# A two-layer hybrid decoder on one core: last sums of the output projection in other banks, earlier copies at the joint, and a plane of four added squares

## What is computed

```
def _layer(x, ...):
    x = _layer_norm(ALPHA * x + 0.5 * _swiglu(x, ffn1...), ln1_g, ln1_b)      # FFN 1, LN1
    xp, q, k, v, xq, gates = jnp.split(x @ w_in, SPLITS, axis=-1)
    ...                      # causal pooling, sliding-window GQA with sinks, cross attention
    merged = sum of sigmoid(gate_b) * (branch_b @ w_br_b) over three branches
    x = _layer_norm(ALPHA * x + merged @ w_o, ln2_g, ln2_b)                   # output projection, LN2
    x = _layer_norm(ALPHA * x + 0.5 * _swiglu(x, ffn2...), ln3_g, ln3_b)      # FFN 2, LN3

def _layer_norm(x, g, b):
    mu = jnp.mean(x, axis=-1, keepdims=True)
    var = jnp.mean(jnp.square(x - mu), axis=-1, keepdims=True)
    return (x - mu) * lax.rsqrt(var + LN_EPS) * g + b
```

## Time and profile before

| what | value |
|---|---|
| time, median of 3 runs | 2475.97 us (2474.82 to 2476.84) |
| the profiled execution's own time | 2475.46 us |
| its span (first to last instruction) | 2472.5 us |
| mean granted TensorE clock | 0.988 of full speed |
| busy share PE / PEld | 97% / 95% |
| busy share DVE / ACT / POOL | 66% / 49% / 25% |
| DMA, mean over the span | 89 GB/s |

### The profile page before, as it was taken

The page is one execution under the profiler, slowest core; times in us unless marked ns, Lnnn a source line. Parts: engine busy times, 40 slices in busy tenths (PEclk is TensorE's granted clock), DMA queues, the critical chain, the costliest instruction groups (busy, mean ns, idle before and its releaser), DMA issues.

```text
span 2472.5 us, 45123 instructions
## 1 busy us (share of the span) xinstructions
PE 2406.2 (97%) x17595; PEld 2341.8 (95%) x17595; DVE 1622.5 (66%) x2744; ACT 1221.0 (49%) x2472; POOL 623.5 (25%) x576
## 2 busy tenths in 40 slices
PE   8999999999999899999999999999999998999997
PEld 8999999899999899999999999989999998999997
DVE  4877776635344587777677777664453457877775
ACT  5555655334322465655565656553443225655654
POOL 1233334120000223333423333341100002333333
PEclk9999999989999999999999999999999999999999
DMA  6222233221122212222213222333112231232231
GB/s 229 93 95 95 95 103 123 77 75 50 61 85 86 86 65 91 89 99 96 93 60 107 93 103 78 112 105 109 43 57 69 86 103 51 73 105 97 84 106 56
DMA packets 54178, 221.29 MB, mean 89 GB/s; under 512 B 15856, under 2 KB 18800, under 8 KB 40880
## 3 DMA queue, kind: packets, MB, share of 16 engines
q1 hardware_dynamic: 53968, 218.41, 26.0%
HBM read 213.58 MB, written 6.04 MB: 89 GB/s over the span
## 4 chain that ended last, share of the span: by engine, by line
PE 79%; DVE 12%; ACT 5%; DVEq 2%; issue 1%; POOL 1%; DMA 0%; ACTq 0%; SPq 0%; POOLq 0%
PE pair L1943 12%; PE pair L1945 11%; PE pair L1944 11%; PE pair L1786 9%; PE pair L1790 9%; PE pair L1788 9%; PE S L1943 2%; PE S L1945 2%; PE S L1944 2%; DVE htl L1202 2%; DVE TP L1122 1%; PE S L2057 1%; ACT hth L743 1%; PE TP L2117 1%; PE S L1897 1%
## 5 line engine op out<-in xcount | busy, mean ns | idle before, releaser
L1943 PE MATMUL pair<-xth,hiA 128*128 128x288 f32 x1216 | 358.6, 295 | 0.4
L1944 PE MATMUL pair<-xtl,hiA 128*128 128x288 f32 x1216 | 358.8, 295 | 0.0
L1945 PE MATMUL pair<-xth,loA 128*128 128x288 f32 x1216 | 358.4, 295 | 0.0
L695 ACT ACTIVATE hiA<-TP 128x512 fp32r<-128x512 f32 (+1 forms) x372 | 194.0, 555 | 205.0 <-DVE TP L1127 125.0
L1691 POOL TENSOR_TENSOR loB<-rawB,hiB 128x512 fp32r<-128x512 f32 (+1 forms) x128 | 161.1, 1259 | 493.6 <-ACT hiB L695 493.5
L1113 DVE TENSOR_TENSOR loA<-TP,hiA 128x512 fp32r<-128x512 f32 (+1 forms) x372 | 235.7, 634 | 17.0 <-ACT hiA L695 14.2
L1108 DVE TENSOR_TENSOR loA<-rawA,hiA 128x1024 fp32r<-128x1024 f32 x96 | 119.1, 1242 | 181.9 <-ACT hiA L682 181.2
L1943 PEld LDWEIGHTS pair<-xth,hiA 128*128 128x128 f32 x1216 | 228.0, 188 | 1.1 <-DVE loA L1113 1.1
L1691 POOL TENSOR_TENSOR loB<-rawA,hiB 128x512 fp32r<-128x512 f32 (+1 forms) x120 | 143.3, 1194 | 340.1 <-ACT hiB L695 340.1
L1945 PEld LDWEIGHTS pair<-xth,loA 128*128 128x128 f32 x1216 | 228.7, 188 | 0.0
L1944 PEld LDWEIGHTS pair<-xtl,hiA 128*128 128x128 f32 x1216 | 228.3, 188 | 0.0
(11 more groups left out here) (388 smaller groups left out, 7046.5 us busy)
## 6 DMA issues: line engine op xcount, KB each, us to landing
rawA<-in_wblk SPq DMA_DIRECT2D x104, 512.0 KB, 3.5
rawA<-in_wg SPq DMA_DIRECT2D x44, 1024.0 KB, 4.8
rawB<-in_wg SPq DMA_DIRECT2D x44, 1024.0 KB, 4.7
rawB<-in_wd SPq DMA_DIRECT2D x24, 768.0 KB, 4.1
rawA<-in_wd SPq DMA_DIRECT2D x24, 768.0 KB, 4.4
rawA<-in_wt_d SPq DMA_DIRECT2D x4, 1024.0 KB, 4.8
rawB<-in_wt_d SPq DMA_DIRECT2D x4, 1024.0 KB, 4.7
mcs<-in_mks SPq DMA_DIRECT2D x2, 2048.0 KB, 11.9
```

Of the source, the lines that this page charges most:

```text
L695: nc.scalar.activation(slot((hiA, hiB), prod, n), src, ACT.Copy).then_inc(f_hi, 1)
L1943: nc.tensor.matmul(bank, wt_hi, xt[0], start=start, stop=False, skip_group_check=True)
L1944: nc.tensor.matmul(bank, wt_hi, xt[1], start=False, stop=False, skip_group_check=True)
L1945: last = nc.tensor.matmul(bank, wt_lo, xt[0], start=False, stop=i == n - 1, skip_group_check=True)
```

## The change

Six edits, all of order, banks or splitting; what is computed stays the same.

1. The memory tokens come in four pieces; the first weight block after the first piece, the second after the fourth. ACT and DVE follow.
2. POOL's add_squares adds the two first sums to one plane (after a drain) and announces only that and 4+5; PE's variance has four matmuls instead of five.
3. At the joint (u == HEADS) ACT's copy_u3 stands ahead of round_hidden(fb, 1, 0) and DVE's sum of c22 ahead of the rest of that hidden plane.
4. Attention: v's transposes go behind project(Q_IN + 3, 0), and the first group's callback comes after chunk 6.
5. Output projection: half 1 of m = 6 and 7 goes to S and TP; residual(4,1) goes ahead of the reciprocal, (5,1) and (6,1) take the places after chunks 1 and 4, (7,1) alone stays at the end. PE's head of FFN 2 waits for the banks only at group 1, and for earlier reads of them.
6. At LN2, PE's mean of half 1 goes into block (1,0,0) after chunk 2 and the variance of half 1 from block (1,0,0) to block (1,1,0), after chunk 5.

```diff
-SQUARE_SUMS = (0, 2, 4)
+SQUARE_SUMS = (0, 4)
...
-            return pair[m % 2][:, 0, 0:TH] if h else (S, TP)[m % 2][:, 1, 0:TH]
+            return (S, TP)[m % 2][:, 1, 0:TH]
...
-            for s in range(2):
-                sp.dma_start(mem[:, 4 * s:4 * s + 4, :], mem0[:, 4 * s:4 * s + 4, :]).then_inc(mem_in[s], 16)
-                sp.dma_start(raw[:, s, :], wblk[s]).then_inc(raw_in[s], 16)
+            for i in range(4):
+                sp.dma_start(mem[:, 2 * i:2 * i + 2, :], mem0[:, 2 * i:2 * i + 2, :]).then_inc(mem_in[i], 16)
+                if i in (0, 3):
+                    sp.dma_start(raw[:, i // 3, :], wblk[i // 3]).then_inc(raw_in[i // 3], 16)
...
-                    if old:
-                        act.wait_ge(f_done, done(fb, u - 1, "P7"))
-                        nc.scalar.activation(u3[:, :], al[(u - 1) % 2], ACT.Copy).then_inc(al_act, 1)
+                    def copy_u3(v):
+
+                        act.wait_ge(f_done, done(fb, v, "P7"))
+                        nc.scalar.activation(u3[:, :], al[v % 2], ACT.Copy).then_inc(al_act, 1)
+
+                    if old and u > HEADS + 1:
+                        copy_u3(u - 1)
...
                     if u == HEADS:
+                        copy_u3(u)
                         round_hidden(fb, 1, 0)
...
+                    if u == HEADS:
+                        sum_c22(u)
...
                     tail_onto_x(fb - 1, 0, 1)
+                else:
+                    residual(4, 1)
                 reciprocal(l, n, 0)
...
-                        residual(4 + c // 4, 1)
+                        residual(5 + c // 4, 1)
...
-                    residual(6, 1)
                     residual(7, 1)
...
-                for c in SQUARE_SUMS:
+                for c in (0, 2, 4):
                     pool.wait_ge(sq_ready, norm_count(l, n, h, c + 1))
-                    nc.gpsimd.tensor_tensor(squares(c), squares(c), squares(c + 1), ALU.add).then_inc(sq_sum, 1)
+                    last = nc.gpsimd.tensor_tensor(squares(c), squares(c), squares(c + 1), ALU.add)
+                    if c == 2:
+                        pool.drain()
+                        last = nc.gpsimd.tensor_tensor(squares(0), squares(0), squares(2), ALU.add)
+                    if c > 0:
+                        last.then_inc(sq_sum, 1)
...
-                    elif f == 1 and g == 0:
-                        pe.wait_ge(pair_free[w], n_use(fb // 2, Q_WO + 3) + 2)
+                    elif f == 1 and g == 1:
+                        pe.wait_ge(pair_free[w], n_use(fb // 2, Q_WO + 2) + 2)
...
-                        if fb and (g, w, h, c) == (1, 0, 0, 5):
+                        if n == 1 and (g, w, h, c) == (1, 0, 0, 2):
+                            mean(l, n, 1)
+                        if fb and (g, w, h, c) == ((1, 1, 0, 5) if n == 1 else (1, 0, 0, 5)):
                             variance(l, n, 1)
...
-                    if fb and h == 0:
+                    if n == 2 and h == 0:
                         mean(l, n, 1)
...
+                project(l, pq(l, Q_IN + 3), 0, n_use(l, Q_IN + 3))
                 pe.wait_ge(pair_free[1], n_use(l, Q_IN + 2) + 2)
...
-                project(l, pq(l, Q_IN + 3), 0, n_use(l, Q_IN + 3))
                 project(l, pq(l, Q_IN + 3), 1, n_use(l, Q_IN + 3))
...
-                        project(l, pq(l, Q_IN + 4), i, n_use(l, Q_IN + 4), between)
+                        project(l, pq(l, Q_IN + 4), i, n_use(l, Q_IN + 4), between, 6 if i == 0 else 4)
...
-                            pe.wait_ge(half_added, l * 4 + m - 5)
+                            pe.wait_ge(half_added, l * 4 + m - 3)
```

More of the change, by code:

```diff
@@ L314, in build @@
         cst_in, x_in, par_in = sem("cst_in"), sem("x_in"), sem("par_in")
-        mem_in = [sem("mem_in0"), sem("mem_in1")]
+        mem_in = [sem(f"mem_in{i}") for i in range(4)]
         raw_in = [sem("raw_in0"), sem("raw_in1")]
@@ L704, in fill_head @@
                     if s == EXTRA:
-                        act.wait_ge(mem_ready, 2)
+                        act.wait_ge(mem_ready, 4)
                     elif s < 4:
@@ L746, in _ @@
             nc.scalar.activation(small[:, 60:61], small[:, 61:62], ACT.Copy)
-            for s in range(2):
-                act.wait_ge(mem_in[s], 16)
-                cs = slice(4 * s, 4 * s + 4)
+            for i in range(4):
+                act.wait_ge(mem_in[i], 16)
+                cs = slice(2 * i, 2 * i + 2)
                 nc.scalar.activation(memh[:, cs, :], mem[:, cs, :], ACT.Copy).then_inc(mem_hi, 1)
-                round_w(0, s)
+                if i in (0, 2):
+                    round_w(0, i // 2)
             for s in range(2):
@@ L1159, in _ @@
             nc.vector.memset(small[:, 60:62], 1.0).then_inc(small_set, 1)
-            for s in range(2):
-                cs = slice(4 * s, 4 * s + 4)
-                dve.wait_ge(mem_hi, s + 1)
+            for i in range(4):
+                cs = slice(2 * i, 2 * i + 2)
+                dve.wait_ge(mem_hi, i + 1)
                 nc.vector.tensor_tensor(meml[:, cs, :], mem[:, cs, :], memh[:, cs, :].bitcast(F32), ALU.subtract).then_inc(mem_ready, 1)
-                rest_w(0, s)
+                if i in (0, 2):
+                    rest_w(0, i // 2)
             for i in range(1, PAIR_MEM):
@@ L1269, in ffn, with sum_c22 @@
                     r, r_old = u % 2, (u - 1) % 2
-                    if g_old:
-                        dve.wait_ge(al_act, 2 * g_count(fb, u - 1))
+                    def sum_c22(v):
+                        dve.wait_ge(al_act, 2 * g_count(fb, v))
                         dve.drain()
-                        nc.vector.tensor_tensor(c22[:, :], u3[:, :], de[r_old], ALU.add).then_inc(de_read, 1)
+                        nc.vector.tensor_tensor(c22[:, :], u3[:, :], de[v % 2], ALU.add).then_inc(de_read, 1)
+                    if g_old and u > HEADS + 1:
+                        sum_c22(u - 1)
                     if d_old:
@@ L1806, in begin, with project @@
                     pe.wait_ge(pair_free[s], u + 1)
-            def project(l, qq, s, u, halfway=None):
+            def project(l, qq, s, u, meanwhile=None, after=4):
                 begin(qq, s, u)
                 for c in range(KC):
-                    if c == KC // 2 and halfway:
-                        halfway()
+                    if c == after and meanwhile:
+                        meanwhile()
                     last = mm3(lambda h: pair[s][:, h, 0:TH], wt(s, c), (xs(xh, c), xs(xl, c)), c, KC)
@@ L1854, in _ @@
                     for c in range(KC):
-                        pe.wait_ge(mem_ready, c // 4 + 1)
+                        pe.wait_ge(mem_ready, c // 2 + 1)
                         last = mm3(lambda h: pair[s][:, 0, 0:N_MEM], wt(s, c, split_of(2 * l)),
```

## The result

The changed kernel takes 2497.16 us (median of 4 runs, 2494.46 to 2499.39) against 2475.39 us before: a ratio of 1.0088, 95% interval 1.0074 to 1.0101, so slower by 22 us (0.9%). The direction is the one forecast, the size is not: +12.1 was forecast, and the range ended at 2495.

A forecast was written before the change was run, and what follows sets the result against it. PE was taken as the bound (79% of the chain's span). Terms -0.4 + 5.3 + 1.6 - 3.8 + 5.4 + 4.0 = +12.1 on 2475.46 gave 2487.6, said as 2488, range 2471 to 2495.

The forecast's parts named there:

- Start and attention: First weight block behind less memory traffic, -0.4; attention's waits for tmp and prob filled, -1.9 in each of two layers, -3.8.
- Joint: P4's wait for u3 goes, but DVE's longer chain delays the next c22: +0.4 at four joints, +1.6.
- Squares: Variances of the norms: one matmul less, but POOL's u comes 0.95 later at six sites PE waits at; together +5.3.
- Head of FFN 2: Mean 3.1 earlier, then PE waits 4.1 for POOL's rests; second reciprocal 2.7 later per layer, +5.4 at full clock.
- Clock: Half rate behind the new 4.1 wait in FFN 2's head: +2.0 in each of two layers, +4.0.
- (a): Rival: same chain, but the clock stays at 2.4 GHz behind the new wait; 2484 (2483 to 2485), chance 0.20.
- (b): Rival: rests of quarters 2 and 3 are there when PE reaches block (1,1,0); -13.8, 2474, chance 0.08.
- (c): Rival: the joints keep their gain, P3's c22 not bound by the chain; -6.0 instead of +1.6, 2480, chance 0.11.
- (d): Rival: every edit gains what it removes, all 27.6 gone; 2448, chance 0.03.

The follow-up runs named there:

- run with the rests ahead: Changed kernel with ACT's rounding and POOL's rests of quarters 2 and 3 put ahead of LN2's second squares: 2483.72 us (1.0033).
- old joint: Changed kernel with edit 3 undone (copy of u3 and sum of c22 at their old places): 2495.58 us (1.0086).
- old head: Changed kernel with edits 5 and 6 undone (old banks, old places of residuals, mean and variance of LN2's second half): 2488.68 us (1.0057).
- plane-alone kernel: Kernel before with edit 2 alone (plane of four squares): 2492.36 us (1.0063).

## Why the prediction was right and wrong

- **Start and attention** (-0.4 and -3.8): right about the waits. In the changed kernel's trace the attention wins 4.35 over both layers. Alone, the two edits measured -2.1, an interval that includes no change, since half-rate stretches in the attention moved; that stood only in the bounds.
- **Joint** (+1.6): right that no gain comes, and in size 0.4 at three of four FFNs by the traces; +1.6 when undone, which the medians alone do not tell from 0. The forecast had one follower that waits 2; there are two that wait 1 each.
- **Squares** (+5.3): the step that failed most. The latency was there: "u comes 0.95 later" holds (415.06 against 414.31 in the earlier trace rows, with POOL starting 0.18 earlier). What failed is "PE's end is POOL's u plus the same three matmuls as before": those matmuls ran at half clock at three of the four first halves of LN1 and LN3 and at the end of the last norm. Before, PE took the sums one by one as they came, so its longest idle piece there was 0.9; with one plane it stands idle 2.4 to 2.6 at a stretch. The clock was weighed at the head of FFN 2 alone, and at the squares not at all. Also wrong was "at LN1 half 1 PE is late by itself ... -0.25": with the plane PE waits there for u too. PE in the changed kernel, LN1's second half, layer 0:

```profile
438.17 0.65 PE L1916 MATMUL S<-hf,cst 128*128 128x288 f32 x2
439.71 0.75 PE L1916 MATMUL S<-u,cst 128*128 128x288 f32 x2 [0.89 <-POOL u L1677]
```

  In place of 5.3, undoing the plane gave 12.4. An estimate of its parts from the traces: 0.9 of latency at LN1's and LN3's first halves and at LN3's second halves, 1.5 of half clock at each of three first halves, 1.2 of half clock at the last norm, and 0.6 to 0.7 at LN1's second halves.
- **Head of FFN 2** (+5.4): the mechanism was right up to the second reciprocal, in layer 0 to some tenths: mean 3 earlier against the head's entry (taken as LN2's first reciprocal), 4.04 of waiting for rests behind the squares, reciprocal 4.6 later against that entry where 2.7 and 2.0 of half clock were forecast. In layer 1 it came 6.1 later: the clock was at 0.50 from 2073.3 on, already in block (1,0,0), and the mean came only 1.5 earlier. The run with the rests ahead confirms that the order is the cause; it moved ACT's rounding and POOL's rests together.
- **Clock** (+4.0): right for the first wait, but the text ended with "Half 1's first chunk ... comes at 866.9; PE has two chunks left and waits the rest", and priced nothing behind that wait of 3.6. A second half-rate stretch stands there in both layers, 6.8 us long; without the plane the stage behind it took 1.0 and 1.3 longer than before. Without the plane the head's two terms would have been 3.5 + 4.0 = 7.5; 11.4 was measured with the start's edit in.
- **Sum.** Undone one at a time the three costly edits give 12.4 + 8.5 + 1.6 = 22.5; all undone together (the run with start and attention alone) 24.3. Forecast for them: 5.3 + 9.4 + 1.6 = 16.3. Between the two profiled executions the last reciprocal is 23.2 later, some 11 more than the +12.1. An estimate of these 11 from the stages of the table and of the experiments: 5.8 is half clock in four variances (three times 1.5, and 1.2 at the last norm), 2.2 stands behind the wait for half 1, 1.4 in layer 1's head, 1.8 at LN1's second halves. By medians, how it divides between squares and head depends on which is undone first, since the new head hides the plane at LN2. Times over 2495 had been given a chance of 0.03, for half rate over twice as much work with no gain in the attention; half rate did come over more work, at places that had no term, and the attention kept its gain.
- **Rivals.** (a), that the clock holds, is refuted by the windows; (b) needs the rests ahead of the squares, which the change doesn't do; given them, the run is 13.4 faster than the changed kernel, and (b) stood 13.8 below the forecast. (c) is refuted by the old joint, and (d), 2448, by the result.

## What to carry to other kernels

Price a new wait of the bound engine twice: its length, and what the matmuls behind it cost if the clock has fallen, at every place that gets one and not only at the longest. An addition that saves the bound engine one short matmul is no saving when the slow engine that makes it is waited for; taking the pieces as they come, with the late one last, won 0.27 at each variance that waits, where gathering them cost 12 to 17 us in all. When a stall is removed, follow the in-order programs of the helpers (here POOL's squares ahead of its rests): the time goes to whoever stands behind them.

## What was not expected of the hardware

TensorE was granted 1.2 GHz after waits as short as 2.5 us (LN3's first half, 0.50 from 1237.1 to 1240.5), while in the kernel before a wait of 2.3 left it at 1.00, and a wait of 2.58 in the changed kernel at 415.25 did too. The length of the wait alone doesn't tell which: the kernel with the old head is the same program up to that place, waits 2.60 there, and is granted 0.50:

```profile
415.60 1.30 PE L1915 MATMUL S<-hf,cst 128*128 128x288 f32 x2 [2.60 <-POOL hf L1679]
...
415.20:418.60 3.40, 3.00 (x6) 2.15 (x7) 0.00 (x0) 0.00 (x0) 1.75 (x3) 0.50 0.10 40
```

In the five traces with the plane and without useless matmuls the clock fell at 16 of the 20 first halves of LN1 and LN3, for 1.3 to 1.5 us each. What decides between them isn't shown. Useless matmuls in such a wait paid for themselves in the plane-alone kernel, 1.3 to 1.5 us at each first half where the clock had fallen without them; in the wait of 2.4 for half 1 they kept the clock at 1.00 and the trace shows no gain.
